# Two fused transformer blocks on one core: another order of the modulation blocks in the first mixer, and of output products, transposes and copies in the second block

## The chip, the core and the metric

The kernel runs on one core of a Trainium2 chip. The metric is the device time of one execution in microseconds, the median of several runs. All data are float32.

## The reference, cut to what matters

Two transformer blocks of two layers each follow one another on the same 256 tokens of width 1024.

```python
# first block, per layer: modulation, a pooling/attention mixer, a mixture of experts
mod = (silu(c) @ w_ada[l] + b_ada[l])              # 6 x 1024 values from a 24 MB weight
h = rms_norm(x, norm1_g[l]) * (1.0 + sc1) + sh1    # then pooling + window attention, w_out
x = x + g1 * (y @ w_out[l])
h2 = rms_norm(x, norm2_g[l]) * (1.0 + sc2) + sh2
# 8 heads pick 16 experts each: 128 rows of u and of v per token
x = x + g2 * peer_ffn(h2, ...)                     # sum_e gelu(h2 . u[e]) * gate[e] * v[e]
# second block, per layer: four mixers a, b, c, d, then a squared-relu MLP
...
mix = jnp.concatenate([rms_norm_2(y_a, out_g_mla[l]), y_b,
                       rms_norm_2(y_c, out_g_swa[l]), rms_norm_2(y_d, out_g_na[l])], axis=-1)
x = x + mix @ w_out[l]
h = rms_norm_2(x, norm2_g[l])
x = x + jnp.square(jax.nn.relu(h @ w_up[l])) @ w_down[l]
```

## The kernel before

Every engine has its own program, in an order written out by hand; semaphores join them. `pe` is TensorE, `v` VectorE, `a` ScalarE; POOL and SP only issue DMAs. "t" is one of the two halves of 128 tokens.

**The first block.** `drive` sets the order on TensorE, VectorE and ScalarE alike. It counts steps k; at each step the mixer's generator `pre` goes on to what stands at that step in the table `WHEN` (scores of two head groups at s0 and s1 = 34, their transposes of the exponentials at pT0 = 36 and pT1 = 40, values at 41 and 45, transposes T1 at 53, output products at 57, 59, 61 and 63, the last transposes T2 at 74), and behind it, when k is in the tuple `MEANWHILE`, the generator `early` does one thing more of its own. `early` multiplies the weight of the modulation. That weight comes in 48 blocks of 1 MB, 24 for each layer. POOL loads them in a ring of nine slots, in which later the experts' rows go too: block b + 9 is asked for when TensorE has multiplied block b. For blocks 0 to 23 one step of TensorE is `matvec` of the block (16 rows of 32x256 in the trace) and `spread` of the block before, VectorE's step adds the bias (`partial`), ScalarE's step copies the result of the block before (`modulation`). Two PSUM banks take turns, so `matvec` of a block waits for ScalarE's copy of the one two blocks earlier. A step of its own ends each group of blocks (the `spread` of blocks 7, 19 and 23). For blocks 24 to 47 a step is only `row` on TensorE. Nine steps of `early` are done ahead of `MEANWHILE`, and what is left of them goes with the first two heads, which come after the mixer. The first heads give the experts' numbers (`EID`); from then on POOL gathers 4 x 128 pieces of 1 MB (line 505), one for each pair of 128 tokens and an expert's place, each read by VectorE (line 1770) and multiplied by TensorE. The ring's rule holds for them too.

**The second block.** In each layer ten groups of attention, called here g0 to g9 (d0, d1, d2, d3, m0, m1, w0, w1, n0, n1 in the code's `ORDER`), run through a pipeline of rounds r: TensorE makes the scores of g(r), the values of g(r-3), a projection of this round if there is one (C1 at r = 2, D1 at 6, D2 at 9), and the transposes of g(r-2). VectorE takes maxima and biases of g(r-1), sums of g(r-2), scales values of g(r-3) and copies transposes of g(r-2); ScalarE has the exponentials and its share of the copies. Then `mixed_T` transposes the mixed output of a section (a, b, c or d), an engine copies it to HT, and `out2` multiplies it with its part of the output weight into banks 0 and 1 for t = 0, and 2 and 3 for t = 1 (4 matmuls of 128x512 each). When all four sections of a t are summed, VectorE adds them to X, ScalarE squares, VectorE scales, and TensorE transposes H (`transposes`) for `widen`, the first product of the MLP. Both layers do the same.

## Time and profile before

| | us |
|---|---|
| median of three runs | 2308.43 (2305.83 to 2312.58) |
| the profiled execution, its own time | 2297.69 |
| its span, first to last instruction | 2295.9 |
| TensorE busy | 2058.7 (90%) |
| VectorE busy | 1338.5 (58%) |
| ScalarE busy | 828.6 (36%) |
| mean granted clock of TensorE | 0.976 |

The profile is of one execution. Busy shares are means over stages with different limits, so the table says little on what limits which stage; the trace is read stage by stage. All times inside the kernel are microseconds from the start of the span. In the rows, "x16" is a number of instructions, and the brackets at the end say how long the engine stood idle before and what ended that.

### The profile page before, as it was taken

The page shows a single profiled execution, that of the slowest core. Times are in us where ns is not written, and L with a number is a line of the kernel's source. Part 1 is how long each engine was busy: PE and PEld are TensorE (multiplying, and loading weights), DVE is VectorE, ACT ScalarE, POOL GpSimd, SP SyncE. Part 2 cuts the span into 40 slices and gives each one's busy share as a digit, 9 for nine tenths or more (in the row PEclk, how much of TensorE's full clock was granted, in tenths as well). Part 3 has the DMA queues.
Part 4 walks back from the last instruction along what each step waited for, and adds up shares of the span by engine and source line. Part 5 has one row for each costly group of instructions (what it writes and reads, how often), then busy time and mean ns, then how long its engine had stood idle before and what let it go on. Part 6 is the DMA issues. An engine that isn't in the chain of part 4 may idle for free.

```text
span 2295.9 us, 24261 instructions
## 1 busy us (share of the span) xinstructions
PE 2058.7 (90%) x8172; PEld 1226.1 (53%) x8172; DVE 1338.5 (58%) x3057; ACT 828.6 (36%) x2389; POOL 609.2 (27%) x564
## 2 busy tenths in 40 slices
PE   6898998897979888999887888889999999999998
PEld 5564554453535434655443243436757666766665
DVE  2237867988557677786778566754524332544323
ACT  2224644545354344464444444542420001331000
POOL 1124445344444343433443444330000000000000
PEclk9898999998999999999999999999999999999999
DMA  9899999999999999999999999994342342242430
GB/s 372 362 419 427 418 426 426 427 426 422 426 427 422 426 427 424 427 385 427 426 427 421 426 427 427 426 427 182 128 184 110 156 182 71 105 189 93 185 152 19
DMA packets 106017, 750.82 MB, mean 327 GB/s; under 512 B 12034, under 2 KB 12322, under 8 KB 16035
## 3 DMA queue, kind: packets, MB, share of 16 engines
q0 software_dynamic: 80640, 587.24, 60.9%
q1 hardware_dynamic: 25252, 162.03, 17.8%
q8 instruction: 65, 1.06, 0.2%
q14 instruction: 60, 0.49, 0.1%
HBM read 748.17 MB, written 1.05 MB: 326 GB/s over the span
## 4 chain that ended last, share of the span: by engine, by line
PE 54%; DMA 22%; DVE 15%; ACT 6%; issue 2%; POOL 1%; DVEq 0%; ACTq 0%; POOLq 0%
PE PS L565 52%; DMA BIG<-in_uv,EID 18%; DVE BIG L1770 6%; DMA MOD<-in_uv,EID 2%; ACT DG L1044 1%; DMA BIG<-in_wada 1%; ACT L1257 1%; DVE BIG L1424 1%; ACT L1248 1%; DVE BIG L1434 1%; DVE SC L1516 1%; PE PS L677 1%; ACT AV L1044 1%; DVE BIG L1420 1%; PE PS L644 1%
## 5 line engine op out<-in xcount | busy, mean ns | idle before, releaser
L565 PE MATMUL PS<-BIG,DG 128*128 128x512 f32 (+1 forms) x2156 | 898.5, 587 | 152.4 <-ACT DG L1044 129.7
L1770 DVE CUSTOM_DVE_ANT_0 BIG<-BIG,H 128x1024 f32<-128x1024 f32 x455 | 558.2, 1227 | 305.5 <-DMA BIG<-in_uv,EID 276.7
L505 POOL DMA_INDIRECT BIG<-in_uv,EID x455 | 521.9, 1147 | 721.0 <-PE PS L565 691.8
L565 PEld LDWEIGHTS PS<-BIG,DG 128*128 128x128 f32 (+1 forms) x2156 | 341.0, 182 | 607.9 <-issue 305.4
L565 PE MATMUL PS<-HT,BIG 128*128 128x128 f32 (+1 forms) x2304 | 383.9, 323 | 10.4 <-DMA BIG<-in_wq 5.3
L565 PEld LDWEIGHTS PS<-HT,BIG 128*128 128x128 f32 x2304 | 349.5, 193 | 75.2 <-issue 45.1
L1257 ACT ACTIVATE AV<-AV 128x1 f32<-128x1 f32 x512 | 103.1, 201 | 609.4 <-DVE AV L1770 602.4
L565 PE MATMUL PS<-BIG,HT 128*128 128x256 f32 (+3 forms) x1216 | 292.4, 397 | 7.3 <-DVE HT L1424 3.6
L565 PEld LDWEIGHTS PS<-BIG,HT 128*128 128x128 f32 x1216 | 224.6, 191 | 73.0 <-issue 46.2
L1424 DVE TENSOR_TENSOR BIG<-BIG 128x256 f32<-128x256 f32 (+2 forms) x176 | 96.1, 546 | 221.7 <-ACT BIG L1396 216.5
L1044 ACT ACTIVATE DG<-CST,AV 128x128 f32<-128x128 f32 x512 | 205.5, 401 | 48.5 <-ACT AV L1044 1.1
L565 PE MATMUL PS<-BIG 128*128 128x512 f32 (+6 forms) x504 | 164.9, 499 | 1.7 <-DVE BIG L1420 1.7
L1044 ACT ACTIVATE AV<-AV,GATE 128x1 f32<-128x1 f32 x512 | 150.7, 294 | 18.8 <-ACT AV L1257 0.4
L1396 ACT ACTIVATE BIG<-PS 128x512 f32<-128x512 f32 x32 | 19.1, 597 | 350.5 <-PE PS L565 350.5
L565 PE MATMUL PS<-MOD,DG 128*128 128x512 f32 (+1 forms) x276 | 113.9, 569 | 16.8 <-ACT DG L1044 16.7
L565 PEld LDWEIGHTS PS<-BIG 128*128 128x128 f32 (+3 forms) x504 | 79.5, 190 | 66.6 <-issue 62.8
L1770 DVE CUSTOM_DVE_ANT_0 BIG<-MOD,H 128x1024 f32<-128x1024 f32 x57 | 70.1, 1229 | 36.5 <-DMA MOD<-in_uv,EID 32.9
L1044 ACT ACTIVATE BIG<-PS 128x256 f32<-128x256 f32 (+6 forms) x122 | 53.1, 448 | 87.0 <-PE PS L677 46.7
L565 PEld LDWEIGHTS PS<-MOD,DG 128*128 128x128 f32 (+1 forms) x276 | 43.1, 181 | 77.0 <-issue 39.6
L565 PE MATMUL PS<-MOD,BIG 128*128 128x64 f32 (+1 forms) x320 | 81.8, 401 | 1.8 <-DVE BIG L1420 1.7
L505 POOL DMA_INDIRECT MOD<-in_uv,EID x57 | 61.6, 1081 | 75.0 <-PE PS L565 69.6
L565 PEld LDWEIGHTS PS<-MOD,BIG 128*128 128x128 f32 x320 | 47.6, 191 | 37.1 <-issue 36.0
(191 smaller groups left out, 1418.1 us busy)
## 6 DMA issues: line engine op xcount, KB each, us to landing
BIG<-in_wada POOLq DMA_DIRECT2D x43, 1024.0 KB
BIG<-in_wup SPq DMA_DIRECT2D x32, 1024.0 KB, 8.9
BIG<-in_wdn SPq DMA_DIRECT2D x32, 1024.0 KB, 4.9
BIG<-in_win SPq DMA_DIRECT2D x31, 1024.0 KB, 5.0
BIG<-in_wout SPq DMA_DIRECT2D x24, 1024.0 KB, 5.5
BIG<-in_wq SPq DMA_DIRECT2D x23, 1024.0 KB
BIG<-in_uv,EID POOLq DMA_INDIRECT x455
MOD<-in_wada POOLq DMA_DIRECT2D x5, 1024.0 KB
```

The costliest lines, as they stand in the source:

```text
L505: pool.e.indirect_dma_start(out=slot(u), out_offset=None, in_=I[f"uv{l}"], in_offset=bass.IndirectOffsetOnAxis(ap=EID[:, t * 128 + j:t * 1 ...
L565: return pe.e.matmul(dst, a, b, start=start, stop=stop)
L644: p = pe.e.transpose(PS[:, bk, c * 128:(c + 1) * 128], H[:, t, (c4 * 4 + c) * 128:(c4 * 4 + c + 1) * 128], ident)
L677: p = pe.e.transpose(PS[:, bk, x * 128:(x + 1) * 128], P[:, i, kc * 128:(kc + 1) * 128], ident)
L1044: return a.e.activation(dst, src, ACT.Copy, scale=scale)
L1248: a.e.activation(GATE[:, j:j + 16], V[:, 32:48], ACT.Exp, bias=V[:, 48:49], scale=1.0, accum_out=V[:, 49:50]).then_inc(*up("a.gate", l, t, h))
L1257: a.e.activation(AV[:, j:j + 1], AV[:, j:j + 1], ACT.Gelu).then_inc(*up("a.gelu", p, b - 1))
L1420: return v.e.tensor_copy(dst, src)
L1424: return v.e.tensor_tensor(dst, a, b, op)
L1434: return v.e.scalar_tensor_tensor(out=dst, in0=a, scalar=s, in1=b, op0=op0, op1=op1)
L1516: v.e.reduce_max(mx, src, AX).then_inc(*up("v.c"))
L1770: v.e.tensor_tensor_reduce(out=JD, in0=slot(u)[:, 0:1024], in1=H[:, t, :], scale=1.0, scalar=0.0, op0=ALU.mult, op1=ALU.add, accum_out=AV[ ...
```

## The change

The table `MEANWHILE` gets five steps more at 34, 35, 37, 40 and 41 and loses 58, 60 and 62. So block 19 is multiplied at step 34 (before: 36), block 20 at 36 (42), 21 at 37 (44), 22 at 39 (46), 23 at 40 (48), and blocks 24 to 29 at 42 to 52 (before: 52 to 62). No block is left between the four output products, and ten instead of twelve go with the heads.

In the second block, in both layers, the projection D2 is cut in two halves around the transposes of g7. The eight products `out2` no longer stand section by section, but so that another product or transpose is between a section's transposes and its first product; all of t = 0 is complete two products before the last of t = 1. The `transposes` of t = 0 stand ahead of the last product of t = 1, those of t = 1 between the first two `widen` products. On VectorE the copy of projection C1 goes from round 2 to round 3, behind the maxima and sums there, and the squares of the b section in round 7 go behind the copy of g5's transposes. No arithmetic is added or taken away.

```diff
--- before.py
+++ after.py
@@ -38,7 +38,7 @@
 BATCH = {(1, 8): (0, 1), (1, 20): (1, 0)}
 PROJ = (2, 3, 4, 0, 1)
 
-MEANWHILE = (15, 16, 17, 18, 19, 20, 24, 27, 29, 31, 33, 36, 39, 42, 44, 46, 48, 50, 52, 54, 56, 58, 60, 62, 65, 68, 70, 72, 73, 76)
+MEANWHILE = (15, 16, 17, 18, 19, 20, 24, 27, 29, 31, 33, 34, 35, 36, 37, 39, 40, 41, 42, 44, 46, 48, 50, 52, 54, 56, 65, 68, 70, 72, 73, 76)
 
 BEHIND = (), (0,), (1,), (2, 3), (4,)
 
@@ -854,10 +854,11 @@
                     bk = singles.where[("prj", l, name)] = FIRST[l][name]
                     if l > 0:
                         pe.wait_ge(*at("v.xf", l - 1, 0))
-                else:
+                elif 0 in parts:
                     bk, freed = singles.take(("prj", l, name), (EVAC[name] + ".prj", l, name))
                     if freed:
                         pe.wait_ge(*at(*freed))
+                bk = singles.where[("prj", l, name)]
                 for z in parts:
                     zs = slice(z * 128, (z + 1) * 128)
                     for k in range(8):
@@ -1006,26 +1007,32 @@
                     elif r == 6:
                         project(l, "D1")
                     elif r == 9:
-                        project(l, "D2")
+                        project(l, "D2", (0,))
                     elif r == 10:
                         mixed_T(l, "b")
                         mixed_T(l, "a")
                     if r > 1:
                         p_transposes(groups[r - 2], p_views(in_2, groups[r - 2])[0])
+                    if r == 9:
+                        project(l, "D2", (1,))
                     if r > 9:
-                        for t in range(2):
-                            out2(l, "b" if r == 10 else "a", t)
+                        out2(l, "b", r - 10)
+
                 values(groups[9], p_views(in_2, groups[9])[1])
                 mixed_T(l, "c")
-                for t in range(2):
-                    out2(l, "c", t)
+                out2(l, "a", 0)
                 mixed_T(l, "d")
-                for t in range(2):
-                    out2(l, "d", t)
-                for t in range(2):
-                    transposes(2 + l, t, 2, ("v.n2", l, t))
-                    widen(l, 0, (t,))
-                    widen(l, 1, (t,))
+                out2(l, "c", 0)
+                out2(l, "d", 0)
+                out2(l, "a", 1)
+                out2(l, "c", 1)
+                transposes(2 + l, 0, 2, ("v.n2", l, 0))
+                out2(l, "d", 1)
+                widen(l, 0, (0,))
+                transposes(2 + l, 1, 2, ("v.n2", l, 1))
+                widen(l, 1, (0,))
+                widen(l, 0, (1,))
+                widen(l, 1, (1,))
                 for q in range(8):
                     for part in range(2):
                         if q < 7:
@@ -1968,10 +1975,10 @@
                     elif r == 2:
                         for t in range(2):
                             evac_heads("mT", MT, 1, 4, 4, 96, l, t)
-                        projected(l, "C1")
                     elif r == 3:
                         for t in range(2):
                             v.wait_ge(*at("pe.dT", l, t))
+                        projected(l, "C1")
                         v.wait_ge(*at("a.prj", l, "C0"))
                         wc, ws = turns(64, 32)
                         tmp = RT[:, 0:768].rearrange("p (t n) -> p t n", t=2)
@@ -1985,12 +1992,6 @@
                         if r < 5:
                             v.wait_ge(*at("pe.hT", 2 + l, groups[r - 3].t, 0, 1))
                         attended(groups[r - 3])
-                    if r == 7:
-                        yb = Y[:, :, 256:512].rearrange("p t (i d) -> p t i d", i=4)
-                        jb = RT[:, 0:512].rearrange("p (t i d) -> p t i d", t=2, i=4)
-                        tt(jb, yb, yb, ALU.mult).then_inc(*up("v.c"))
-                        own()
-                        v.e.reduce_sum(sc("yb", 8), RT[:, 0:512].rearrange("p (i d) -> p i d", i=8), AX).then_inc(*up("v.subs", l))
                     if r == 9:
                         scaled(l, "a")
                         q = inverse("yb", 8, ("yb", l)).rearrange("p (t i) -> p t i", t=2)
@@ -2000,6 +2001,12 @@
                         ins.then_inc(*up("v.yn2", l, "b"))
                     if r > 1:
                         evac_pT(groups[r - 2], in_2)
+                    if r == 7:
+                        yb = Y[:, :, 256:512].rearrange("p t (i d) -> p t i d", i=4)
+                        jb = RT[:, 0:512].rearrange("p (t i d) -> p t i d", t=2, i=4)
+                        tt(jb, yb, yb, ALU.mult).then_inc(*up("v.c"))
+                        own()
+                        v.e.reduce_sum(sc("yb", 8), RT[:, 0:512].rearrange("p (i d) -> p i d", i=8), AX).then_inc(*up("v.subs", l))
                 scaled(l, "c")
                 attended(groups[9])
                 scaled(l, "d")
```

The first place is TensorE in the first mixer, steps 34 to 41. `BIG,TC` is a modulation block, `ACC,ONES` a spread, `CST,BIG` the transposes of a head group's exponentials. Before:

```order
L565 MATMUL PS<-BIG 128x128 [waits v_bias]
L565 MATMUL PS<-BIG 128x128 x3
L677 MATMUL PS<-CST,BIG 128x128 [waits a_exp]
L677 MATMUL PS<-CST,BIG 128x128 x3
L565 MATMUL PS<-BIG,TC 32x256 [waits ga1,a_ada]
L565 MATMUL PS<-BIG,TC 32x256 x7
L565 MATMUL PS<-ACC,ONES 128x256 [waits v_part] x2
L677 MATMUL PS<-CST,BIG 128x128 [waits a_exp]
L677 MATMUL PS<-CST,BIG 128x128 x3
L565 MATMUL PS<-PRJ,BIG 128x64 [waits a_pT,v_pw]
L565 MATMUL PS<-PRJ,BIG 128x64 x3
```

And now:

```order
L565 MATMUL PS<-BIG 128x128 [waits v_bias]
L565 MATMUL PS<-BIG 128x128 x3
L565 MATMUL PS<-BIG,TC 32x256 [waits ga1,a_ada]
L565 MATMUL PS<-BIG,TC 32x256 x7
L565 MATMUL PS<-ACC,ONES 128x256 [waits v_part] x2
L677 MATMUL PS<-CST,BIG 128x128 [waits a_exp]
L677 MATMUL PS<-CST,BIG 128x128 x3
L565 MATMUL PS<-BIG,TC 32x256 [waits ga2,a_ada]
L565 MATMUL PS<-BIG,TC 32x256 x7
L565 MATMUL PS<-BIG,TC 32x256 [waits ga3,a_ada]
L565 MATMUL PS<-BIG,TC 32x256 x7
L565 MATMUL PS<-ACC,ONES 128x256 [waits v_part]
```

Blocks 19 to 23 now stand around the two groups of transposes, where before there was one block between them.

The second place is TensorE at the end of the attention, layer 0, from the values of g9 on. `BIG,HT 128x512` are `out2` products (4 rows each), `MOD,BIG` the values of g9, `CST,H` transposes (in line 907, now 908: `mixed_T`; in line 644: `transposes`). Before:

```order
L565 MATMUL PS<-MOD,BIG 128x64 [waits v_pT,a_pT]
L565 MATMUL PS<-MOD,BIG 128x64 x7
L907 MATMUL PS<-CST,H 128x128 [waits v_yn2,v_att]
L907 MATMUL PS<-CST,H 128x128 x3
L565 MATMUL PS<-BIG,HT 128x512 [waits a_yT,ld9]
L565 MATMUL PS<-BIG,HT 128x512 x7
L907 MATMUL PS<-CST,H 128x128 [waits v_yn2]
L907 MATMUL PS<-CST,H 128x128 x3
L565 MATMUL PS<-BIG,HT 128x512 [waits v_yT,ld10]
L565 MATMUL PS<-BIG,HT 128x512 x7
L644 MATMUL PS<-CST,H 128x128 [waits v_n2]
```

And now, from the second product of section b on, which stands ahead of those values:

```order
L565 MATMUL PS<-BIG,HT 128x512 [waits v_bias]
L565 MATMUL PS<-BIG,HT 128x512 x3
L565 MATMUL PS<-MOD,BIG 128x64 [waits v_pT,a_pT]
L565 MATMUL PS<-MOD,BIG 128x64 x7
L908 MATMUL PS<-CST,H 128x128 [waits v_yn2,v_att]
L908 MATMUL PS<-CST,H 128x128 x3
L565 MATMUL PS<-BIG,HT 128x512 [waits ld8]
L565 MATMUL PS<-BIG,HT 128x512 x3
L908 MATMUL PS<-CST,H 128x128 [waits v_yn2]
L908 MATMUL PS<-CST,H 128x128 x3
L565 MATMUL PS<-BIG,HT 128x512 [waits a_yT,ld9]
L565 MATMUL PS<-BIG,HT 128x512 x3
```

Behind each group of transposes there is now a product that doesn't read them.

The third place is VectorE, layer 0, rounds 2 and 3. `COPY MOD<-PS 128x2x256` is the copy of C1; `TENSOR_REDUCE` takes the maxima of g2; the `SCALAR_TENSOR_TENSOR` rows end with what lets TensorE transpose g1. Before:

```order
L1420 COPY BIG<-PS 96x4x128 [waits v_mT,pe_mT]
L1420 COPY MOD<-PS 128x2x256 [waits v_mT,pe_prj]
L1516 TENSOR_REDUCE SC<-PS 128x4 [waits pe_score]
L1429 TENSOR_SCALAR SC<-SC 128x4 [waits v_c]
L1534 RECIPROCAL SC<-SC 128x4 [waits a_exp]
L1430 TENSOR_SCALAR BIG<-BIG,SC 128x256 [waits v_c]
L1434 SCALAR_TENSOR_TENSOR BIG<-BIG,SC 128x256 [waits v_c]
L1430 TENSOR_SCALAR BIG<-BIG,SC 128x256
L1434 SCALAR_TENSOR_TENSOR BIG<-BIG,SC 128x256 [waits v_c]
L1424 TENSOR_TENSOR G<-MOD,CST 128x2x6x32 [waits v_lam,a_prj]
```

And now:

```order
L1427 COPY BIG<-PS 96x4x128 [waits v_mT,pe_mT]
L1523 TENSOR_REDUCE SC<-PS 128x4 [waits pe_score]
L1436 TENSOR_SCALAR SC<-SC 128x4 [waits v_c]
L1541 RECIPROCAL SC<-SC 128x4 [waits a_exp]
L1437 TENSOR_SCALAR BIG<-BIG,SC 128x256 [waits v_c]
L1441 SCALAR_TENSOR_TENSOR BIG<-BIG,SC 128x256 [waits v_c]
L1437 TENSOR_SCALAR BIG<-BIG,SC 128x256
L1441 SCALAR_TENSOR_TENSOR BIG<-BIG,SC 128x256 [waits v_c]
L1427 COPY MOD<-PS 128x2x256 [waits v_lam,pe_prj]
L1431 TENSOR_TENSOR G<-MOD,CST 128x2x6x32 [waits v_prj,a_prj]
```

The copy, which waits for TensorE's projection, went behind the work on g1 and g2, and stands right ahead of the rotation (`G<-MOD,CST`) that reads it.

## Rows read from the trace of the kernel before

**Rows 1.** Page of the profile: DMA share in 40 equal slices, tenths.

```profile
DMA  9899999999999999999999999994342342242430
```

**Rows 2.** Busy times by stretch; last three columns PEclk, DMA share, GB/s.

```profile
96.00:120.00 24.00, 18.80 (x146) 10.95 (x142) 8.48 (x28) 8.44 (x28) 3.17 (x6) 0.72 0.69 261
100.00:112.00 12.00, 9.01 (x52) 5.65 (x56) 3.17 (x13) 4.12 (x18) 0.53 (x1) 0.50 0.43 150
...
180.00:1525.00 1345.00, 1181.95 (x3818) 613.93 (x3818) 985.36 (x2386) 647.00 (x1873) 568.46 (x496) 0.97 1.01 424
1656.00:1660.00 4.00, 4.00 (x21) 3.13 (x20) 3.46 (x9) 2.60 (x11) 0.00 (x0) 0.57 0.00 0
```

**Rows 3.** Timeline of POOL (DMA issues) in the first mixer.

```profile
103.92 0.53 POOL L498 DMA_DIRECT2D BIG<-in_wada  x1 [6.51 <-PE PS L565]
112.89 0.53 POOL L498 DMA_DIRECT2D BIG<-in_wada  x1 [8.45 <-PE PS L565]
...
168.56 0.98 POOL L505 DMA_INDIRECT BIG<-in_uv,EID  x1 [4.71 <-DVE EID L1434]
```

**Rows 4.** Timeline of TensorE in the first mixer: start, duration, idle before.

```profile
97.11 1.16 PE L565 MATMUL PS<-BIG 64*128 64x128 f32 x8
100.61 1.11 PE L677 MATMUL PS<-CST,BIG 128*128 128x128 f32 x4 [2.35 <-ACT BIG L1120]
101.65 1.94 PE L565 MATMUL PS<-BIG,TC 128*32 128x256 f32 x16
...
123.59 1.96 PE L644 MATMUL PS<-CST,H 128*128 128x128 f32 x8 [2.80 <-DVE H L1429]
...
142.05 3.72 PE L565 MATMUL PS<-BIG,HT 128*128 128x256 f32 x16
...
151.04 1.09 PE L644 MATMUL PS<-CST,H 128*128 128x128 f32 x8 [0.81 <-DVE H L1424]
...
177.85 1.94 PE L565 MATMUL PS<-BIG,DG 128*32 128x256 f32 x16 [0.50 <-DMA BIG<-in_wada]
```

**Rows 5.** Timeline of ScalarE in the first mixer.

```profile
119.49 0.62 ACT L1081 ACTIVATE HT<-H 128x512 f32<-128x512 f32 x1
```

**Rows 6.** Timeline of TensorE in the second block, layer 0.

```profile
1622.95 0.66 PE L677 MATMUL PS<-CST,BIG 128*128 128x128 f32 x4 [1.47 <-DVE BIG L1434]
...
1654.52 2.09 PE L565 MATMUL PS<-PRJ,BIG 128*128 128x64 f32 x16 [2.09 <-DVE BIG L1420]
...
1661.94 7.13 PE L565 MATMUL PS<-BIG,HT 128*128 128x256 f32 x32
...
1670.81 1.97 PE L565 MATMUL PS<-MOD,BIG 128*128 128x64 f32 x16 [0.87 <-DVE BIG L1420]
...
1695.07 7.10 PE L565 MATMUL PS<-BIG,HT 128*128 128x512 f32 x16 [1.02 <-ACT HT L1044]
...
1703.48 7.11 PE L565 MATMUL PS<-BIG,HT 128*128 128x512 f32 x16 [0.87 <-DVE HT L1424]
1711.03 1.09 PE L644 MATMUL PS<-CST,H 128*128 128x128 f32 x8 [0.44 <-DVE H L1429]
...
1722.12 7.38 PE L565 MATMUL PS<-HT,BIG 128*128 128x128 f32 x64 [0.87 <-ACT HT L1044]
```

**Rows 7.** Timelines of VectorE, then ScalarE, second block, layer 0.

```profile
1618.98 0.69 DVE L1420 COPY MOD<-PS 128x512 f32<-128x512 f32 x1 [6.58 <-PE PS L565]
...
1646.49 0.69 DVE L1420 COPY BIG<-PS 128x512 f32<-128x512 f32 x1 [7.87 <-PE PS L565]
...
1653.68 0.69 DVE L1420 COPY BIG<-PS 128x512 f32<-128x512 f32 x1
...
1659.47 0.57 ACT L1044 ACTIVATE BIG<-PS 128x512 f32<-128x512 f32 x1
```

**Rows 8.** Timeline of TensorE in the second block, layer 1.

```profile
1988.96 0.66 PE L677 MATMUL PS<-CST,BIG 128*128 128x128 f32 x4 [1.47 <-DVE BIG L1434]
...
2061.09 7.11 PE L565 MATMUL PS<-BIG,HT 128*128 128x512 f32 x16 [1.02 <-ACT HT L1044]
```

## The prediction

> **What bounds the kernel now.** I read the page first. DMA is full in nearly all of the first 27 of 40 slices and mostly under half busy after them [rows 1]: the first block lives by transfers, the second by something else. The table by stretch sharpens it: from 180 to 1525 us, the experts' gathers, the share is 1.01 at 424 GB/s, with TensorE and VectorE both less than full [rows 2]. What starts the gathers earlier ends the first block earlier by as much. Then I looked at what comes ahead of them: one hole. From 96 to 120 us only 261 GB/s moved [rows 2]. Against 424 that is 24 x (1 - 261/424) = 9.2 us of transfers missing. Its maker stands in POOL's timeline: it waited 6.5 and 8.5 us for TensorE before the requests at 103.92 and 112.89 [rows 3], because one modulation block alone was multiplied between about 97 and 110 us; all nine slots had landed. The first gather is asked for at 168.56 after a wait for EID [rows 3], but modulation blocks are still landing then: TensorE waits for the last one at 177.85 [rows 4]. So at 168 the mixer's own chain is early by some 9 us, and transfers are late.
>
> In the second block TensorE works 90% and more, and what is left are short waits, each named at its row: the chain there goes through TensorE's program and these waits [rows 6], the same in layer 1, shown by two of them [rows 8].
>
> **The change, first mixer.** Nothing is added; 1 MB takes 1.05/424 = 2.47 us. Block 19 now follows the second group's scores, which end at 98.2 (97.11 + 1.16, less the overlap), and falls in the 2.35 us for which TensorE stood idle before 100.61 [rows 4], with both spreads. Its refill is asked for at 99.3 instead of 103.9. Block 20 waits for ScalarE's copy for block 18, which stands behind the first exponentials; it comes after the transposes of 100.61, thus ends at 102.4 to 103.6 (16 rows take 1.94 at the half rate that the clock has here [rows 2, 4], about half at full). Blocks 21, 22 and 23 follow at about 104, 105.5 and 109, 24 and 25 at 112 and 113. Refills so asked for keep the transfers going but for 0 to 1.2 us at the second one; I take 0.6.
>
> The mixer's own chain: ScalarE's squares, which wait for the second group's values, began at 119.49 [rows 5]. These values now follow block 25 at 112.8 and take 1.0, VectorE's scaling 0.4: squares at 114.3. T1 came 4.1 after them (123.59 - 119.49), so at 118.4; with 1.0 for T1 at full rate and 1.9 for blocks 30 and 31 the products begin at 121.3. Four of 3.65 to 3.72 [rows 4] with no block between end at 136.0, and T2 follows after 5.3 as before (145.7 to 151.04): 141.3, and EID at about 159. That gives no time by itself, since the last modulation block lands at about 169. But it has a price to check: from 121.3 to 137.5 no block is multiplied and no refill is asked for, 16.2 us. At 121.3 refills are out to block 40, and (121.3 - 101.4)/2.47 = 8 MB have landed since block 27, two of them output weights: 34 to 40 are still under way, 17.3 us of transfers, and SP's loads (about 3.5 MB, 8.6 us) besides. DMA doesn't run dry. Sum: 9.2 - 0.6 = **8.6 us**; bounds 6 (further gaps of the 1.2 us kind) and 9.2.
>
> **The change, second block, per layer.**
> - C1's copy: VectorE stood 6.58 us until 1618.98 for TensorE's projection [rows 7], with g2's maxima and g1's sums queued behind it; TensorE then waited 1.47 for them before transposing g1 [rows 6]. Now they lie in those 6.58 us. What is late next is ScalarE's exponentials of g2, behind its copy for g0: about 0.1. The rotation starts 3.2 us earlier and no longer holds the next transposes. Gain 1.4; it reaches the end, since VectorE's busy stretch from 1646.49 on begins with a wait of 7.87 us for TensorE [rows 7].
> - The squares in round 7: the copy at 1653.68 [rows 7] moves up 1.5 us, so the values at 1654.52 lose 1.5 of their 2.09 us wait [rows 6]. But the next values need ScalarE's copy of 1659.47 [rows 7], which stands behind the exponentials of g7, and these behind VectorE's bias of g7, whose time doesn't change. Gain 0: the wait moves to the front of 1660.1 and becomes 3.2 us long.
> - D2 in two halves (7.13 whole [rows 6]): VectorE's copy for g7 gets done under the second half. ScalarE's doesn't: it stands behind the copy of D2, and D2 now ends 1 us later. The values start about 0.35 later than at 1670.81, in place of the wait of 0.87; VectorE absorbs most of it. Loss 0.15.
> - The order of output products and transposes: each 3.5 us product now covers a copy or a norm. The waits of 1.02, 0.87, 0.44 and twice 0.87 (1712.99, whose row is not shown, and 1722.12) go: 4.07 [rows 6]. One comes: the norm of t = 1 takes as long as that of t = 0 did, 1711.03 - (1703.48 + 3.55) = 4.0, and one widening, 7.38/2 = 3.69, covers it: 0.35. Section c's and d's norms on ScalarE and VectorE end before TensorE gets there (1685 and 1690.6 against 1686.8 and 1690.9, in times of before; d is tight). Gain 3.7.
> - The clock. After the wait of 2.09 us the stretch from 1656 to 1660 ran at a mean of 0.57 [rows 2], part of it at 1.2 instead of 2.4 GHz; that cost nothing, because TensorE had to wait until 1660.1 anyway. Now a longer wait stands right ahead of D2, whose products nothing covers. The same 4 x (1 - 0.57) = 1.7 us may be lost there, or 0 if the lower level comes at another moment. I take half, 0.85.
>
> The Trainium skill ("TensorE: Matmul & The Clock Gate", "Why this matters for your kernels") says to avoid idle gaps between bursts of matmuls, because the clock goes back to its half rate after them. By that rule the longer wait costs the 1.7 us in both layers, and the whole forecast would be 1.7 us higher; the row shows a drop after the shorter wait too, which agrees with the rule.
>
> Per layer 1.4 + 3.7 - 0.15 - 0.85 = 4.1, in both **8.2 us**; bounds 3.3 and 5.0 per layer. Hidden edits cost nothing as long as TensorE's program is behind ScalarE's and VectorE's there; without that cover section d's transposes would wait up to 1 us.
>
> **Sum.** 8.6 + 8.2 = 16.8 us. The profiled execution took 2297.7, its span 2295.9; they should become 2280.9 and 2279.1. The runs' median lies 10.7 us above the profile, and I carry the difference over: 2308.4 - 16.8 = **2291.6 us**.
>
> **Rivals.**
> 1. *The hole in the transfers only moves.* The four products in a row free no slot for 16.2 us. If DMA had nothing left at 121.3 but SP's 8.6 us, 7.6 us would be idle and the first mixer would give 1. Against it: 7 blocks under way by the count above. Time: 2308.4 - 1 - 8.2 = 2299.
> 2. *The second block gives nothing:* removed waits come back at ScalarE, which does the copies and norms in strict order (section d's margin is 0.3 us), and at the clock. Against it: each wait's releaser is at its row, and the new orders leave 3.5 us. Time: 2308.4 - 8.6 = 2299.8.
> 3. *Slower, by the clock.* The 3.2 us wait before 1660.1 leaves TensorE at the lower level for long, as in the first mixer, where 100 to 112 ran at 0.50 with TensorE three quarters busy [rows 2]. Each microsecond at half rate costs 0.5. Without any clock loss the gain is 18.5; to end slower by 0.3% (6.9 us) it takes 25.4 us, so 25 us at half rate in each layer. As long as the stretch in the mixer (12 us) it costs 12 us: 2301.9. Against it: TensorE is full behind the wait, and came back from 0.57 within 4 us.
> 4. *The change doesn't do what it says:* the hole in the transfers isn't on the path, because the gathers' start hangs on EID, and the waits move: 2308. Against it: the wait for a modulation block at 177.85.
> 5. *More:* no gap at the second refill, no clock loss, and the mixer at full rate: 9.2 + 10 = 19.2, 2289.
>
> **How the numbers follow.** The forecast, between 14 and 18.5 us of gain, gets 0.62 (2290 to 2295); rival 1 0.09, rival 2 0.12, rival 3 0.05 (0.03 of it slower, the rest no change), rival 4 0.05, rival 5 0.07. The three runs of before span 2305.8 to 2312.6, so 0.3%, 6.9 us, is about what a measurement can tell from no change. Rivals 1 and 2 lie just beyond it at 2299 and 2300. Faster: 0.62 + 0.07 + 0.17 of rivals 1 and 2 = 0.86; same 0.04 + 0.05 + 0.02 = 0.11; slower 0.03. The range leaves out rivals 3 and 4 and takes in the scatter of a median, 3 us: 2286 to 2300.
>
> **What would show it.** In the first mixer: GB/s near 420 from 96 to 120, POOL's waits for TensorE under 4 us there, T1 at about 118, T2 at about 141, the first gather's product at about 174 instead of 182.8, and the gathers' end earlier by as much. In the second block: no wait of VectorE for C1 ahead of g2's maxima; no 1.47 wait; a wait of about 3 us before the values of g6 and then D2's first half slow or not; under 0.5 us of waits from there to the MLP. The forecast is wrong if the share of DMA falls under 1 between 125 and 170 us, if EID comes after the last modulation block, or if section d's transposes wait.

## The result and the profile after

The changed kernel takes 2283.24 us, the median of four runs (2281.14 to 2284.11); four runs of the kernel before beside it have a median of 2308.01. The ratio is 0.9894, with a 95% interval of 0.9867 to 0.9922: 24.5 us less (18 to 31). The forecast was 2291.6 with a range of 2286 to 2300. The direction was right, the size too small by 8 us, and the time lies under the range. One profiled execution against the other says much less than the runs: the span went from 2295.9 to 2282.3, 13.6 us. Why these two numbers, 24.5 and 13.6, differ is the question of this case.

The page of the changed kernel shows the share of DMA in 40 slices, against [rows 1]:

```profile
DMA  8999999999999999999999999995342342342430
```

Its table by stretch, with the columns of [rows 2] (last three: granted clock, DMA share, GB/s):

```profile
96.00:120.00 24.00, 21.56 (x251) 12.67 (x251) 9.94 (x32) 10.98 (x34) 6.55 (x12) 1.00 1.01 413
100.00:112.00 12.00, 10.58 (x112) 5.63 (x104) 5.98 (x19) 5.87 (x26) 2.64 (x5) 1.00 1.00 405
180.00:1525.00 1345.00, 1177.94 (x3819) 611.19 (x3818) 981.69 (x2379) 644.95 (x1871) 562.05 (x498) 0.98 1.01 423
```

The hole is closed: 413 GB/s instead of 261 [rows 2], and with it the clock came back, 1.00 instead of 0.50 from 100 to 112. The experts' stretch is as it was. POOL's timeline, against [rows 3]:

```profile
101.01 0.53 POOL L498 DMA_DIRECT2D BIG<-in_wada  x1 [2.19 <-PE PS L565]
104.01 0.53 POOL L498 DMA_DIRECT2D BIG<-in_wada  x1 [2.48 <-PE PS L565]
...
110.32 0.53 POOL L498 DMA_DIRECT2D BIG<-in_wada  x1 [2.74 <-PE PS L565]
...
137.75 0.53 POOL L498 DMA_DIRECT2D BIG<-in_wada  x1 [14.48 <-PE PS L565]
...
159.21 0.98 POOL L505 DMA_INDIRECT BIG<-in_uv,EID  x1 [8.56 <-DVE EID L1441]
```

No wait over 3 us in the place of those of 6.51 and 8.45. The wait of 14.48 under the output products is there too and costs nothing; the last row is the first gather, asked for at 159.21 instead of 168.56. TensorE in the first mixer, against [rows 4]:

```profile
122.34 14.08 PE L565 MATMUL PS<-BIG,HT 128*128 128x256 f32 x64
...
141.68 1.09 PE L644 MATMUL PS<-CST,H 128*128 128x128 f32 x8 [0.81 <-DVE H L1431]
...
165.56 1.94 PE L565 MATMUL PS<-BIG,DG 128*32 128x256 f32 x16 [2.62 <-DMA BIG<-in_wada]
```

T2 comes at 141.68 instead of 151.04, and the products wait for modulation blocks after it: the mixer's chain is early and transfers are late, as before. Lines are 7 higher now in this part of the code (L1441 was L1434).

TensorE in the second block, layer 0, against [rows 6]:

```profile
1647.19 2.25 PE L565 MATMUL PS<-PRJ,BIG 128*128 128x64 f32 x16 [1.69 <-ACT BIG L1051]
1649.24 1.92 PE L677 MATMUL PS<-CST,BIG 128*128 128x128 f32 x8
...
1653.17 2.00 PE L565 MATMUL PS<-MOD,BIG 128*128 128x64 f32 x16 [0.42 <-ACT BIG L1051]
1655.01 3.67 PE L565 MATMUL PS<-BIG,HT 128*128 128x256 f32 x16
...
1664.23 2.17 PE L565 MATMUL PS<-MOD,BIG 128*128 128x64 f32 x16 [1.22 <-issue]
...
1669.45 3.60 PE L565 MATMUL PS<-BIG,HT 128*128 128x512 f32 x8
1672.88 1.89 PE L565 MATMUL PS<-MOD,BIG 128*128 128x64 f32 x16
...
1707.06 1.09 PE L644 MATMUL PS<-CST,H 128*128 128x128 f32 x8 [0.30 <-DVE H L1436]
```

The wait of 1.47 is gone, the one of 2.09 is 1.69 and now ends on ScalarE's copy, the 0.87 ahead of the values of g7 became 1.22, and behind them one short wait, 0.30, is left where there were six: the five that the sum counts and one of 0.78 at 1674.87. Eight transposes that take 1.04 at full rate took 1.92 at 1649.24, so the clock is at half rate here as it was in the kernel before.

### The profile page after: what moved, and what is told of

It is laid out like the page before. It is cut to its first block, busy times and chain, and to the rows that moved or that the text cites. A ratio compares the mean times of both kernels' runs of the same rounds, so it can differ in the third digit from the quotient of the medians.

```text
span 2282.3 us, 24261 instructions
## 1 busy us (share of the span) xinstructions
PE 2052.8 (90%) x8172; PEld 1225.7 (54%) x8172; DVE 1338.6 (59%) x3057; ACT 827.7 (36%) x2389; POOL 602.4 (26%) x564
## 4 chain that ended last, share of the span: by engine, by line
PE 54%; DMA 23%; DVE 15%; ACT 6%; issue 2%; POOL 0%; DVEq 0%; ACTq 0%; POOLq 0%
PE PS L565 52%; DMA BIG<-in_uv,EID 20%; DVE BIG L1777 6%; DMA MOD<-in_uv,EID 2%; DMA BIG<-in_wada 1%; ACT DG L1051 1%; ACT L1264 1%; DVE BIG L1431 1%; ACT L1255 1%; ACT AV L1051 1%; PE PS L644 1%; ACT BIG L1127 1%; DVE BIG L1427 1%; PE PS L677 1%; DVE BIG L1441 1%
## 5 line engine op out<-in xcount | busy, mean ns | idle before, releaser
L505 POOL DMA_INDIRECT BIG<-in_uv,EID x455 | 513.9, 1129 | 733.5 <-PE PS L565 700.3
## 6 DMA issues: line engine op xcount, KB each, us to landing
MOD<-in_wada POOLq DMA_DIRECT2D x5, 1024.0 KB, 13.7
```

Of the source, the lines that this page charges most:

```text
L505: pool.e.indirect_dma_start(out=slot(u), out_offset=None, in_=I[f"uv{l}"], in_offset=bass.IndirectOffsetOnAxis(ap=EID[:, t * 128 + j:t * 1 ...
```

## The experiments

Times are medians of the timed runs in us; each ratio is to runs of the kernel before on the same chip. Four chips were used, and the medians of before on them lie between 2305.1 and 2309.0, so kernels from different chips are better compared by their ratios than by their medians.

| kernel | median | runs | ratio, 95% interval |
|---|---|---|---|
| kernel before (22 runs beside the next four kernels) | 2305.89 | 2298.2 to 2316.0 | 1 |
| kernel before again | 2305.99 | 2302.0 to 2317.0 | 1.0003, 0.9986 to 1.0020 |
| table of blocks alone | 2294.99 | 2292.5 to 2309.2 | 0.9961, 0.9942 to 0.9981 |
| second block alone | 2289.53 | 2287.0 to 2294.7 | 0.9936, 0.9914 to 0.9957 |
| changed kernel | 2281.93 | 2280.1 to 2283.6 | 0.9899, 0.9879 to 0.9919 |
| before, scores of g3 twice | 2301.40 | 2298.9 to 2307.9 | 0.9977, 0.9964 to 0.9990 |
| before, scores of g3 twice, of g8 three times | 2300.83 | 2298.1 to 2306.3 | 0.9977, 0.9963 to 0.9991 |
| C1's copy alone | 2296.37 | 2294.2 to 2301.5 | 0.9958, 0.9941 to 0.9975 |
| order of products alone | 2295.79 | 2287.4 to 2299.1 | 0.9939, 0.9916 to 0.9961 |
| one more block early | 2283.25 | 2281.5 to 2287.9 | 0.9911, 0.9884 to 0.9938 |
| changed, steps 58, 60, 62 kept | 2283.79 | 2282.4 to 2284.3 | 0.9905, 0.9879 to 0.9931 |
| changed, without halves and squares' move | 2281.44 | 2278.6 to 2282.9 | 0.9898, 0.9872 to 0.9924 |
| D2 spread, first try | 2282.22 | 2281.4 to 2282.7 | 0.9900, 0.9874 to 0.9926 |
| changed, C1's copy back | 2282.76 | 2281.1 to 2294.0 | 0.9903, 0.9874 to 0.9932 |
| D2 spread, second try | 2291.80 | 2289.6 to 2294.4 | 0.9934, 0.9909 to 0.9960 |

The names A to F in the expectations are those of theories that each expectation states itself. Three matter later: theory C says that short waits of TensorE cost mainly by the half rate that follows them, rival D that a wait costs its own length and no more, and theory E that the first block ends earlier by the transfers that are no longer missing.

### The two halves, and the kernels themselves again

**The kernel before again**, no edit.

> The kernel before, once more, to see how its profiled execution stands to its timed ones. Theory A (the profiled execution of before with 2297.7 us was an early outlier or had other conditions than its timed runs, and nothing of the kernel explains it): a new profile comes out at 2306 to 2312 us, where the timed runs are, with the extra 10 us visible as lower GB/s in some stretch of the trace. Theory B (the profiled execution is always some 10 us faster than the timed ones for this kernel): the new profile is near 2298 us again and the timed runs near 2308.

**The table alone**, the line `MEANWHILE` of the diff and nothing else.

> The new table for the modulation blocks alone, the second block as before. Both theories: the hole in the transfers at 96 to 120 us closes. Theory A: the time falls by 8 to 10 us against before, by profile and by timed runs alike (the two halves add up to 16 to 17, and before's median lay high by chance or conditions). Theory B: before has 10 us in its timed runs that its profile does not have, at the hole in the transfers; then this kernel gains 18 to 20 us in timed runs and the second block's part 5 or so.

**The second block alone**, all of the diff but that line.

> The second block's change alone, with the table of modulation blocks as before. Theory A: 7 to 10 us faster than before (5.3 us were seen in layer 0 between the two profiles). Theory B, if the unprofiled 10 us lie in the second block: 18 us faster; if they lie at the hole in the transfers: 8 us faster and timed runs 10 us above its profile.

**The changed kernel again**, no edit.

> The changed kernel once more, beside its two halves. If the halves are independent its gain is their sum within 2 us: 16 to 17 us by theory A, some 25 us by theory B. Its profiled execution lay at 2284.1, its timed runs at 2281 to 2284; both should come again within 3 us.

The kernel before scatters over 18 us, from 2298 to 2316, the changed one over 3.6. The new profiled execution of before took 2301.97, between the first one and the median, so neither theory A nor B is right as it stands: a profiled execution is one draw from a wide lot, and the first one, 2297.69, was a lucky draw: of the 94 timed or profiled runs of before on record here two were lower, and their median is 2306.5. The table gives 9 us alone (by the ratio; the interval is 4 to 13) and 7.6 on top of the second block (2289.53 - 2281.93). The second block gives 15 alone (10 to 20) and 13.1 on top of the table. It is the second block that gave more than the 8.2 of the sum.

The scatter goes with the clock. Of 90 runs of before the mean granted clock is on record: the 30 with the lowest (0.965 to 0.971) have a median of 2310.4, the 30 with the highest (0.973 to 0.979) one of 2302.7.

Where the scatter sits, TensorE's timeline of the kernel before, run again, shows, layer 0:

```profile
1622.50 0.66 PE L677 MATMUL PS<-CST,BIG 128*128 128x128 f32 x4 [1.47 <-DVE BIG L1434]
1622.99 2.99 PE L565 MATMUL PS<-BIG 96*128 96x256 f32 x8
1625.77 1.81 PE L565 MATMUL PS<-MOD,BIG 128*128 128x64 f32 x8
...
1628.65 7.97 PE L565 MATMUL PS<-HT,BIG 128*128 128x256 f32 x32
```

In the first profile the same three products took 1.89, 1.00 and 7.07, with the same wait of 1.47 ahead of them:

```profile
1623.45 1.89 PE L565 MATMUL PS<-BIG 96*128 96x256 f32 x8
1625.18 1.00 PE L565 MATMUL PS<-MOD,BIG 128*128 128x64 f32 x8
...
1626.79 7.07 PE L565 MATMUL PS<-HT,BIG 128*128 128x256 f32 x32
```

The wait is the same and the clock behind it is not: the same products take 2.99 instead of 1.89. That gave theory C.

### Filling a wait with work that does nothing

**The scores of g3 twice**, in the kernel before:

```diff
-            def scores(g):
+            def scores(g, times=1):
...
-                for i in range(g.n):
+                for i in list(range(g.n)) * times:
...
-                        scores(g)
+                        scores(g, 2 if r == 3 else 1)
```

> The kernel before, with the scores of g3 in the second block computed twice in each layer: 1.1 us of work more per layer, right ahead of the 1.47 us wait for VectorE, which it fills but for 0.4 us. No work is taken away. Theory C (the short waits cost mainly by what the clock does behind them: in one profile of the kernel before the stretch behind this wait ran at full rate, in another 6.8 us of it at half rate): the median falls by 2 to 4 us and the highest runs by more. Rival D (a wait costs its own length and no more): no change within 0.5 us, or up to 1 us slower.

**The scores of g8 three times too**: `scores(g, {3: 2, 8: 3}.get(r, 1))`.

> As the kernel that repeats the scores of g3, and the scores of g8 are computed three times, 2.1 us of work more, which fill the 2.09 us wait ahead of the values of g5. Theory C: 4 to 8 us faster than before although 3.2 us of work per layer were added, since neither wait is followed by a half-rate stretch any more; spread of the runs below 8 us. Rival D: no change, or 0 to 2 us slower.

In the first of them the timeline shows the wait nearly filled, and full rate behind it:

```profile
1619.67 2.10 PE L565 MATMUL PS<-BIG 32*128 32x256 f32 x16
1621.70 1.10 PE L565 MATMUL PS<-MOD,BIG 128*128 128x64 f32 x8
1623.31 0.66 PE L677 MATMUL PS<-CST,BIG 128*128 128x128 f32 x4 [0.51 <-DVE BIG L1434]
1623.81 1.89 PE L565 MATMUL PS<-BIG 96*128 96x256 f32 x8
```

With 2 us of products added and none taken away the kernel is 5.3 us faster (2.3 to 8.3), and its lowest run is not lower than those of before. So what became rarer are the bad executions. Rival D, by which a wait costs its own length, gives no gain here and falls. But the profile doesn't show half rate gone, only moved: this execution was the slowest of its twelve (2307.9), had 24 us at half rate in the two attention parts, at other places than behind the filled wait, and they took 164.4 and 177.9 us, as long as in slow executions of before. That the filled wait lowers the median is shown; by which stretches it does so isn't.

Filling the wait of 2.09 as well gave nothing more, against what theory C said. In its profile half rate even came behind the 0.51 us that are left of the first wait, in one of its two layers. What is left at the second wait may be why there is no more gain: in both kernels' profiles a wait of 1.66 for ScalarE stands two operations further on, which the repeats don't fill.

### Parts of the second block's change

**C1's copy alone.**

```diff
-                        projected(l, "C1")
                     elif r == 3:
                         for t in range(2):
                             v.wait_ge(*at("pe.dT", l, t))
+                        projected(l, "C1")
```

> Of the whole change only the move of VectorE's copy for C1 behind the maxima and sums. By the prediction's sum it gives 1.4 us in each layer, 2.8 us. Theory C: these 2.8 us and the clock's losses behind the removed wait, together 5 to 8 us in the median. Rival D: 2.8 us, within the runs' scatter.

**The order of products, transposes and widenings alone**, from `if r > 9:` to the last `widen` of the diff.

> Of the whole change only the order of the output products, transposes and first widenings in both layers. The prediction's sum: 3.7 us per layer, 7.4 us. Theory C and rival D say the same, since no half-rate stretch was seen behind the four waits that it removes: 7 to 8.5 us. If it gives over 10, the clock's losses lie (also) here.

C1's copy gave 9.7 us (6 to 14) where its wait is worth 3, and the order 14 (9 to 19). What the order is worth without the clock can be read off: from the first output product of section b to the first MLP product that waits 0.78 us, TensorE takes 54.9 us in all eight layers of before that were profiled, and 50.2 or 50.3 in the six of the changed kernel and the two of the order alone. Layer 0, before and then the order alone:

```profile
1675.36 7.03 PE L565 MATMUL PS<-BIG,HT 128*128 128x512 f32 x16
...
1730.28 7.14 PE L565 MATMUL PS<-HT,BIG 128*128 128x256 f32 x32 [0.78 <-ACT BIG L1396]
```

```profile
1684.67 3.60 PE L565 MATMUL PS<-BIG,HT 128*128 128x512 f32 x8
...
1734.87 7.14 PE L565 MATMUL PS<-HT,BIG 128*128 128x256 f32 x32 [0.78 <-ACT BIG L1400]
```

That is 4.7 us per layer, 9.4 in both. It lies inside the interval of the timed gain, so an excess over it isn't shown for the order; for C1's copy it is, as theory C has it. Together the two would make 24, and the whole second block gives 15 to 16. If both medians are right, both reach into the same loss.

### The first mixer

**One more block early**, the second block as changed:

```diff
-MEANWHILE = (15, 16, 17, 18, 19, 20, 24, 27, 29, 31, 33, 34, 35, 36, 37, 39, 40, 41, 42, 44, 46, 48, 50, 52, 54, 56, 65, 68, 70, 72, 73, 76)
+MEANWHILE = (15, 16, 17, 18, 19, 20, 24, 27, 29, 31, 33, 34, 36, 39, 42, 44, 46, 48, 50, 52, 54, 56, 58, 60, 62, 65, 68, 70, 72, 73, 76)
```

> The second block as changed, but of the table only one step more than before, at 34, so that blocks 19 and 20 are multiplied at 34 and 36 and all later ones one step of the old table earlier. Theory E (the first block ends earlier by as many microseconds as transfers are less missing at 96 to 120 us, 2.47 us for each megabyte): about one block, 2.5 us, of the 8.5 us; the first gather's product some 2 to 3 us earlier than with the old table. Rival F (it hangs on the mixer's own chain, whose transposes T1 and T2 come earlier with the new table): T1 hardly moves, so gain 0 to 1 us.

**Steps 58, 60 and 62 kept**: `..., 54, 56, 58, 60, 62, 65, ...` in the changed kernel's table.

> The changed kernel with steps 58, 60 and 62 kept, so that three blocks are multiplied between the output products again and three fewer with the heads. Theory E: T2 and EID come 3 to 4 us later, at some 145 and 163 us, which costs nothing since the last modulation block still lands at about the same time; same time as the changed kernel within 1 us. Rival F: 3 to 4 us slower.

The table by stretch of the first:

```profile
96.00:120.00 24.00, 18.05 (x190) 10.90 (x183) 8.15 (x24) 10.53 (x36) 4.75 (x9) 1.00 0.97 377
```

and of the second, with POOL's first gather:

```profile
120.00:180.00 60.00, 47.42 (x417) 31.38 (x415) 27.64 (x84) 12.06 (x24) 15.97 (x18) 0.89 0.99 408
```

```profile
164.66 0.99 POOL L505 DMA_INDIRECT BIG<-in_uv,EID  x1 [22.18 <-DVE EID L1441]
```

One block more at step 34 closed the hole not by 2.5 us but by 6.5: 24 x (1 - 377/424) = 2.7 us are missing instead of 9.2, and the clock stayed at its full rate there; I take it that all that follows came sooner by that, but no run parts the two. The time followed the transfers, 6.3 us less than the second block alone (2289.5 to 2283.3). So theory E fits for what transfers are worth, and my count of one block for one step was wrong. The other kernel closed the hole wholly, and lost elsewhere what I had put at nothing: POOL had asked for every block and waited 22 us for EID, and 60 x (1 - 408/425) = 2.4 us of transfers went missing. Its median is 1.5 us above that of the changed kernel's 14 runs, on another chip, which alone would not tell. The profiles say the same: from T1 to the first transposes of the second block it took 1449.1 us, against 1446.1, 1447.7 and 1446.5 in the changed kernel's three. So taking the blocks from between the products is, by all signs, no idle part of the change: the experts' numbers must be there when the last blocks are.

### D2's halves and the squares

**The changed kernel without them.**

```diff
                     elif r == 9:
-                        project(l, "D2", (0,))
+                        project(l, "D2")
...
-                    if r == 9:
-                        project(l, "D2", (1,))
```

and the five lines of `yb` and `jb` ahead of `evac_pT` in round 7 again.

> The changed kernel without two of its edits: D2 in one piece again, and the squares of section b back ahead of the copy of g5's transposes. The prediction's sum: 0.15 us per layer less without the halves, 0 for the squares, and the clock's 0.85 us per layer not lost: 0 to 2 us faster than the changed kernel. If the edits help after all, 0.5 to 2 us slower.

> The changed kernel without the halves of D2 and the move of the squares, beside the changed kernel on the same chip. In the profiles its layer 0 took 153.1 us against 154.1; if that holds in both layers it is 2 us faster in the median. If the difference is under 1 us, the two edits are worth nothing that a run can tell.

> The changed kernel again, as the companion of the kernel without the two edits: 2281 to 2284 us, 22 to 25 us below before, its runs within 4 us of each other.

On one chip it took 2280.15 against 2281.86 (ratios 0.9881 and 0.9887); over all runs 2281.4 (10) against 2282.3 (14). That is a microsecond at most, less than these runs can tell. The two edits bring nothing; I would leave them out.

**D2's halves at the waits**, in the changed kernel:

```diff
+                    if r == 9:
+                        project(l, "D2", (1,))
+                    elif r == 10:
+                        mixed_T(l, "b")
                     if r > 2:
                         values(groups[r - 3], p_views(in_2, groups[r - 3])[1])
...
-                    elif r == 9:
+                    elif r == 8:
                         project(l, "D2", (0,))
...
                     if r == 9:
+                        projected(l, "D2")
                         squares(l, "a", ("m0", "m1"))
...
+                    if r in (7, 8):
+                        evac_pT(groups[r - 2], in_2)
                     if 1 <= r <= 10:
                         softmax(groups[r - 1], in_2)
```

> The changed kernel with D2's halves put where TensorE waits: the first in round 8 between the values of g5 and the transposes of g6, the second in round 9 ahead of the values of g6, the transposes of section b ahead of the values of g7; ScalarE copies the transposes of g5 and g6 ahead of the exponentials, and D2 ahead of its squares. The waits of 1.69, 2.03 (or 0.42 behind a half-rate stretch) and 1.22 us become about 0.6, 0 and 0.3: 3.5 to 4 us less per layer, 7 to 8 us faster than the changed kernel, 2274 to 2276 us. Theory C adds that no half-rate stretch follows there any more, up to 2 us more. Rival: rounds 7 to 9 are bound by VectorE (6.0 us per round against 4.2 of TensorE), and the waits only move: 0 to 3 us.

**The second try**, on top of it: VectorE copies g7's transposes first in round 9 and section b's first in round 10, and TensorE's transposes of b stand behind the values of g7.

```diff
                 for r in range(12):
+                    if r == 10:
+                        mixed(l, "b")
...
                     if r == 9:
+                        evac_pT(groups[7], in_2)
                         scaled(l, "a")
```

> The kernel with D2's halves in rounds 8 and 9, and on VectorE the copy of g7's transposes ahead of the norms of sections a and b (which stood in front of it, so that TensorE waited 2.96 and 0.97 us), the copy of section b's transposes ahead of the bias of g9, and TensorE's transposes of section b behind the values of g7 again. Waits of 0.6, 1.0 and 0.7 us remain of 0.64, 2.96 and 0.97: 2 to 2.5 us less per layer, 4 to 5 us faster than the first try, 2277 to 2279. If waits appear again in round 10 or 11 instead, rounds 7 to 11 are bound by VectorE as a whole and the time stays at 2281.

TensorE's timeline of the first try, round 10:

```profile
1660.94 0.66 PE L908 MATMUL PS<-CST,H 128*128 128x128 f32 x4 [2.96 <-DVE H L1443]
1662.56 3.65 PE L565 MATMUL PS<-MOD,BIG 128*128 128x64 f32 x16 [0.97 <-ACT BIG L1052]
```

The waits of rounds 8 and 9 went but for 0.64, and the same microseconds stand in round 10: no gain, the rival. The second try made it worse. Its TensorE, and its ScalarE ahead of the copy that TensorE waits for:

```profile
1660.31 3.67 PE L565 MATMUL PS<-MOD,BIG 128*128 128x64 f32 x16 [4.54 <-ACT BIG L1051]
...
1668.98 1.11 PE L677 MATMUL PS<-CST,BIG 128*128 128x128 f32 x4 [2.43 <-DVE H L1432]
```

```profile
1654.61 1.28 ACT L1101 ACT_TABLE_LOAD   x1
...
1656.41 1.28 ACT L1127 ACT_TABLE_LOAD   x1
...
1659.68 0.57 ACT L1051 ACTIVATE BIG<-PS 128x512 f32<-128x512 f32 x1
```

I had moved VectorE's half of g7's copy and left ScalarE's, which stands behind two table loads and the exponentials of g8. A copy that two engines share is as late as the later one. The expectation named VectorE as what could bind; for the wait of 4.54 it was ScalarE's order, while the one of 2.43 behind it does end on VectorE. The waits are not all of the loss either: this profile has 34 us at half rate in the attention parts, the first try's 14.

### Putting the wait back, and the scatter of the kernel before

**C1's copy back in the changed kernel**, the reverse of the edit above.

> The changed kernel with VectorE's copy for C1 put back ahead of the maxima of g2, so that TensorE's wait of 1.47 us in round 3 is there again. Theory C: 1.6 us per layer by the wait itself and more in the median by the half rate behind it, together 6 to 10 us slower than the changed kernel, and runs that lie further apart (changed kernel: 280 to 284) than 5 us. Rival D: 3.2 us slower, 2285 us, and runs as close as the changed kernel's.

**The kernel before, two more profiles**, no edit.

> The kernel before, one more profiled execution. Theory C: its time above 2297 is the time lost in half-rate stretches behind short waits of the second block, 0 to 3 stretches of 1.7 to 3.4 us loss each; the two attention parts take 159.4 to 164.1 and 173.0 to 177.9 us, and the rest of the second block is the same to 0.1 us. Rival: other parts of the execution differ by as much, and the second block's do not.

> The same once more: between the profiled executions of before, the attention parts of the second block differ by up to 10 us, in steps that match the half-rate stretches in the clock's row; the first block by at most 3 us.

The kernel with the copy back has the wait of 1.47 in both layers and full rate right behind it in both. Its median is 2282.8, within 1 us of the changed kernel's runs, and one run in six took 2294. The 6 to 10 us of theory C did not come. The 3.2 of D are not excluded: the mean of the six runs, 2284.7, is 2.7 above that of the changed kernel's 14. A wait is thus not always followed by half rate: I saw it behind the 1.47 us wait in 5 of the 14 layers that have it in the profiles here, and at that place in none of the 22 layers of the kernels without the wait. (With the repeated scores, which leave 0.51 of it, it was one layer of four.)

The two further profiles of before took 2313.30 and 2310.82. What half rate means for the scatter: the first profile of before, by stretch,

```profile
1655.00:1675.00 20.00, 18.31 (x115) 16.06 (x115) 14.02 (x29) 10.97 (x32) 0.00 (x0) 0.91 0.23 92
1992.00:2008.00 16.00, 16.00 (x93) 13.99 (x93) 8.98 (x21) 7.75 (x28) 0.00 (x0) 1.00 0.51 187
2020.00:2048.00 28.00, 25.80 (x136) 20.18 (x137) 15.80 (x32) 13.04 (x40) 0.00 (x0) 0.94 0.39 158
```

and the slowest one (the first of the two further profiles):

```profile
1655.00:1675.00 20.00, 19.07 (x80) 16.58 (x81) 10.73 (x23) 9.06 (x28) 0.00 (x0) 0.66 0.06 24
1992.00:2008.00 16.00, 14.53 (x63) 12.49 (x60) 13.25 (x29) 5.22 (x19) 0.00 (x0) 0.68 0.27 99
2020.00:2048.00 28.00, 25.72 (x132) 21.87 (x131) 17.24 (x35) 11.83 (x37) 0.00 (x0) 0.76 0.30 118
```

A mean of 0.66 over 20 us is (1 - 0.66)/0.5 = 0.68 of it at 1.2 GHz, 13.6 us. In the three stretches together 37 us were at half rate against 7, and the two attention parts took 346.6 us against 332.4: 14.2 us for 30, so 0.47 us for each microsecond at half rate. The other two profiles agree: 4.7 us for 10.2 at half rate, 9.6 for 20.5.

The gain's place can be read off too. Every profile can be cut at the same four rows of TensorE: the first transposes of each layer, and the first product of the MLP that waits 0.78 for ScalarE. Those of before (the second further profile) and of the changed kernel (the last run):

```profile
1574.40 1.09 PE L644 MATMUL PS<-CST,H 128*128 128x128 f32 x8
...
1738.65 1.53 PE L565 MATMUL PS<-HT,BIG 128*128 128x256 f32 x6 [0.78 <-ACT BIG L1396]
...
1931.64 1.09 PE L644 MATMUL PS<-CST,H 128*128 128x128 f32 x8
...
2109.42 7.14 PE L565 MATMUL PS<-HT,BIG 128*128 128x256 f32 x32 [0.78 <-ACT BIG L1396]
```

```profile
1561.33 1.08 PE L644 MATMUL PS<-CST,H 128*128 128x128 f32 x8
...
1715.59 4.77 PE L565 MATMUL PS<-HT,BIG 128*128 128x256 f32 x21 [0.78 <-ACT BIG L1403]
...
1908.58 1.09 PE L644 MATMUL PS<-CST,H 128*128 128x128 f32 x8
...
2076.34 3.91 PE L565 MATMUL PS<-HT,BIG 128*128 128x256 f32 x17 [0.78 <-ACT BIG L1403]
```

| profile | first block | attention, layer 0 | attention, layer 1 | at half rate in both | span |
|---|---|---|---|---|---|
| before, the one shown ahead | 1570.9 | 159.4 | 173.0 | 6.8 | 2295.9 |
| before, again | 1570.4 | 164.1 | 173.0 | 17.0 | 2300.2 |
| before, further 1 | 1572.3 | 164.2 | 182.4 | 37.5 | 2311.5 |
| before, further 2 | 1574.4 | 164.3 | 177.8 | 27.3 | 2309.0 |
| changed | 1565.5 | 154.1 | 170.1 | 13.7 | 2282.3 |
| changed, again | 1565.0 | 156.5 | 167.8 | 13.6 | 2281.8 |
| changed, last | 1561.3 | 154.3 | 167.8 | 13.7 | 2276.0 |
| C1's copy alone | 1571.7 | 157.8 | 171.5 | 6.8 | 2293.6 |
| order of products alone | 1575.5 | 159.4 | 169.8 | 20.5 | 2297.3 |
| scores of g3 twice | 1571.3 | 164.4 | 177.9 | 23.9 | 2306.1 |
| scores of g3 twice, of g8 three times | 1573.7 | 162.6 | 173.1 | 6.8 | 2301.9 |
| changed, C1's copy back | 1563.3 | 155.7 | 172.8 | 20.5 | 2284.4 |
| without halves and squares' move | 1561.1 | 153.1 | 170.1 | 10.2 | 2276.8 |
| the same, again | 1561.3 | 154.6 | 168.2 | 13.7 | 2276.7 |

The column on half rate is worked out from the granted clock in slices of 1 us. Not every stretch costs time: the 3.4 us in layer 1 of the first profile cost nothing that shows, for the kernel with both repeats has none in that layer and takes as long, 173.1 against 173.0.

The MLP between the two parts takes 193.0 in all of them and the rest behind them 199.6. The means of before (1572.0, 163.0, 176.6) less those of the changed kernel (1564.0, 155.0, 168.5) are 8.0, 8.0 and 8.1, together 24.1: the whole gain of the timed runs, with its place. Between the two profiles shown ahead the same three places give 5.4, 5.3 and 3.0, the 13.6 of the spans: the one of before was near the best that this kernel does, and the one of the changed kernel was not.

The first block's spread is made ahead of the change. In the changed kernel's first and last profile TensorE's clock from 20 to 40 us was 0.77 and 1.00, and from 40 to 60 us 327 and 419 GB/s were moved; against 424 that is 4.6 and 0.2 us of transfers missing, and the first blocks differ by 4.2.

## Why the prediction was too slow

**The carried difference is the step that failed.** "The runs' median lies 10.7 us above the profile, and I carry the difference over." The profile on which the sum was made had little half rate in the attention parts, 6.8 us; the typical execution of before has more, some 7 us' worth of time (the mean of the four profiles is 7.1 above the lowest of each layer), and up to 14. So 7.1 of the 10.7 us was not a constant of the measurement but a cost of this kernel in stretches at half rate, which the sum carried over unchanged, that is, put at no gain. The rest of the 10.7 lies in the first block, whose four values spread over 4 us, and in the draw: the three runs with their 2308.4 lay 1.9 above the median of all 94.

The changed kernel is not free of that cost. Without any loss to the clock its layers would take 153.1 and 166.8 (before's best less 1.6 for C1's copy and 4.7 for the order; 153.1 was measured in a kernel without D2's halves). Its three profiles lie 1.8 above that in each layer. The account for the two attention parts, by the means of the profiles, is then 12.5 us for waits (forecast 10.2) and 7.1 of half rate in before gone (forecast 0), less 3.6 of half rate in the changed kernel (forecast 1.7) and nothing for the halves (forecast 0.3): 16.0 together, 16.1 measured, against 8.2. With four and three profiles the terms of the clock are good to a microsecond or two.

**First mixer, 8.6 us: right.** 8.0 by the profiles, 7.6 and 9 by the runs. The hole closed, T1 came at 119.5 (118.4 forecast), T2 at 141.7 (141.3), the first gather was asked for at 159.2 (159). DMA kept its full share under the four products (1.01 and 426 GB/s from 122 to 137 us), so rival 1 is out. The two profiles shown ahead would have given only 5.4, in part because that of the changed kernel had the worst start of its three. The kernel with the three steps kept shows that the second condition, EID ahead of the last block, is close: at 164.7 it seems to cost already.

**Second block, waits: right in kind, small by a fifth.** They gave 6.3 per layer where the sum had 5.1. C1's copy gave 1.6 in each layer (159.4 to 157.8, 173.0 to 171.5; forecast 1.4). The order gave 4.7 in each (54.9 to 50.2, and 157.8 to 153.1 in layer 0; forecast 3.7). The missing 1.0 is how a wait is counted. Rows of TensorE that follow without a wait overlap: 1669.45 + 3.60 = 1673.05, and the next starts at 1672.88, 0.17 earlier. Behind a wait this overlap is lost, and the row itself is longer: 16 products took 7.10 behind the wait of 1.02 [rows 6] and 7.03 at 1675.36 without one. The idle time fell by 4.07 - 0.30 = 3.8, and four fewer waits at 0.17 + 0.07 are 1.0 beside it: 4.7. (The profile models where products end, so this is how its rows add up.) The Trainium skill ("TensorE: Matmul & The Clock Gate", "Step-by-step: what each phase is for") has the same thing as the drain of one product under the fill of the next, and "Single matmul latency" there states about 175 ns for the drain of a bf16 product; this case's 0.17, for float32, agrees.

**D2 in halves, the squares, and the clock there: -1.0 per layer forecast.** 153.1 against 154.1 in layer 0 is that 1.0 in one pair of profiles, but both layers together took 323.0 without the edits (mean of two profiles) and 323.5 with them (of three), and the runs differ by under 1 too. So the cost is about nothing, not 2.0. The 1.0 between 153.1 and 154.1 is half rate behind the wait of 1.22: from D2's start to the first output product the kernel without the edits took 13.4, the changed kernel 14.4 in that profile and 13.4 in layer 0 of its last one, where that stretch ran at full rate. The waits came otherwise than forecast. Those ahead of the values of g5 and g6 were to be 0.6 and 3.2 and were 1.69 and, at full rate, 2.03 (0.42 behind a stretch at half rate), because g5's values then wait for ScalarE's copy, which the squares' move doesn't touch; their sum is as forecast. The wait ahead of g7's values, 0.87 + 0.35, is the 1.22 measured.

**The clock's sign.** I charged the change 0.85 us per layer for half rate and left the kernel before free: of its half-rate stretch I wrote that it "cost nothing, because TensorE had to wait until 1660.1 anyway". In that one execution it was so. In the three other profiles the two attention parts took 4.7, 9.6 and 14.2 us more, with 10.2, 20.5 and 30.7 us more at half rate. The rule of the Trainium skill that I weighed ("TensorE: Matmul & The Clock Gate", "Why this matters for your kernels": no idle gaps between bursts) spoke for the change as a whole, not against it, and I read it only at the one wait that grew. The runs with repeated scores point the same way: a gap filled with idle work gave 5.3 us. But that rule names gaps longer than the 1.47 and 2.09 us behind which half rate came here, so these waits go beyond what it covers.

**Rivals.** 2 (the second block gives nothing), 3 (slower by the clock) and 4 (nothing) are out. Rival 5, more than forecast, is nearest, but its 19.2 us fall short too: it took the clock as a loss that the changed kernel would not have, while the gain came from one that before has. No rival held what happened.

**Open.** C1's copy put back cost 0.5 to 3 us, though alone it gave 9.7. The order alone gave 14 us in the runs, with its waits worth 9 and those of 1.47 and 2.09 left; the interval allows 9, and its profile has 20.5 us at half rate. Why the changed kernel's stretches at half rate make 13.6 to 13.7 us in each profile, and those of before 6.8 to 37.5, isn't shown. Whether half rate follows a short wait depends on more than its length, and the profiles here are too few to say on what.

## What to carry to other kernels

Look at how far the timed runs lie apart before trusting one profile: a kernel that scatters over 18 us with constant work has a cost that this profile may not show, and its median is the place to start from only if one knows whether the change touches that cost. On a TensorE that is nearly full, a wait of 1.5 us ahead of a dense stretch is priced with what the clock may do behind it and with the overlap that it breaks, not by its length alone; repeating a product inside the wait is a cheap test of that. And a copy shared by two engines is moved on both or not at all.
